# Expert gates read from DRAM in groups of eight tiles of 1 KB rows instead of groups of four of 512 B rows

## The reference, cut to what matters

```
s = einsum('thpd,hpnd->thpn', q, subkeys);  sv, si = top_k(s, 16)
comb = sv[:, :, 0, :, None] + sv[:, :, 1, None, :];  cs, ci = top_k(comb, 16)
idx = ia * 128 + ib;   g = softmax(cs)
a = einsum('td,thkd->thk', x, u_tab[idx])
out = einsum('thk,thkd->td', g * gelu(a), v_tab[idx])
```

## Time and profile before

| what | value |
|---|---|
| median of three runs | 1352.08 us (1351.38 to 1352.24) |
| profiled execution, its own time | 1351.97 us |
| its span in the trace | 1350.0 us |
| TensorE matmul busy | 1286.9 us (95%) |
| VectorE busy | 1187.2 us (88%) |
| ScalarE busy | 656.2 us (49%) |
| GpSimd busy | 612.1 us (45%) |
| DMA | 401.89 MB in 153,605 packets, mean 298 GB/s |

### The profile page before, as it was taken

The page is one execution under the profiler, slowest core; times in us unless marked ns, Lnnn a source line. Parts: engine busy times, 40 slices in busy tenths (PEclk is TensorE's granted clock), DMA queues, the critical chain, the costliest instruction groups (busy, mean ns, idle before and its releaser), DMA issues.

```text
span 1350.0 us, 22753 instructions
## 1 busy us (share of the span) xinstructions
PE 1286.9 (95%) x7713; PEld 716.5 (53%) x7713; DVE 1187.2 (88%) x2416; ACT 656.2 (49%) x927; POOL 612.1 (45%) x379
## 2 busy tenths in 40 slices
PE   6999999998865999999989999999999999999997
PEld 3554555455543667777755555555544444444444
DVE  8866398899998999999959989989999898887997
ACT  5652645465534677777634333434343333343442
POOL 4741233466741443344436656757664545222402
PEclk9999999999987999999999999999999999999999
DMA  7232422268765799999999999999999999999972
GB/s 294 95 110 68 136 79 78 94 204 280 236 229 181 264 364 389 388 394 384 407 398 351 394 393 376 400 401 382 364 384 387 375 391 381 391 385 345 386 244 105
DMA packets 153605, 401.89 MB, mean 298 GB/s; under 512 B 12352, under 2 KB 72000, under 8 KB 151360
## 3 DMA queue, kind: packets, MB, share of 16 engines
q1 hardware_dynamic: 112064, 250.06, 51.4%
q0 software_dynamic: 41472, 151.01, 28.9%
HBM read 357.51 MB, written 42.99 MB: 297 GB/s over the span
## 4 chain that ended last, share of the span: by engine, by line
PE 61%; DVE 19%; DMA 10%; issue 7%; ACT 2%; SPq 1%; DVEq 0%; ACTq 0%
PE bank L768 23%; PE bank L756 9%; PE bank L757 9%; PE bank L758 9%; DMA area<-gelu_scratch 3%; DMA raw<-tiles_dram 3%; DMA area<-gates_scratch 2%; PE bank L1033 2%; DVE cut L1442 2%; PE bank L783 2%; DVE ple_gate L1925 1%; DVE area L1686 1%; DVE area L1677 1%; DMA gates_scratch<-area 1%; DVE cut L1449 1%
## 5 line engine op out<-in xcount | busy, mean ns | idle before, releaser
L768 PE MATMUL bank<-cut,area 128*128 128x512 f16 x2208 | 485.0, 380 | 7.4 <-DVE area L1918 5.6
L756 PE MATMUL bank<-hT,cut 128*128 128x352 f16 (+1 forms) x1216 | 395.8, 326 | 34.0 <-DVE cut L1442 25.4
L757 PE MATMUL bank<-hT,cut 128*128 128x352 f16 (+1 forms) x1216 | 395.3, 325 | 0.0
L758 PE MATMUL bank<-hT,cut 128*128 128x352 f16 (+1 forms) x1216 | 395.2, 325 | 0.0
L1064 ACT ACTIVATE cut<-raw 128x1024 f16<-128x1024 f32 x246 | 257.4, 1054 | 233.5 <-DMA raw<-tiles_dram 197.2
L768 PEld LDWEIGHTS bank<-cut,area 128*128 128x128 f16 x2208 | 215.9, 98 | 265.4 <-DVE area L1918 6.2
L1442 DVE SCALAR_TENSOR_TENSOR cut<-raw,cut 128x1024 f16<-128x1024 f32 x198 | 250.2, 1265 | 44.5 <-ACT cut L1064 44.2
L756 PEld LDWEIGHTS bank<-hT,cut 128*128 128x128 f16 x1216 | 119.6, 98 | 114.7 <-DVE cut L1442 25.7
L758 PEld LDWEIGHTS bank<-hT,cut 128*128 128x128 f16 x1216 | 119.8, 98 | 76.6
L757 PEld LDWEIGHTS bank<-hT,cut 128*128 128x128 f16 x1216 | 119.7, 98 | 75.5 <-issue 0.3
L638 POOL DMA_INDIRECT ple_sb<-u_rows_dram,expert_id x64 | 103.5, 1617 | 109.3 <-DVE dots L1653 90.8
(11 more groups left out here) (223 smaller groups left out, 1648.6 us busy)
## 6 DMA issues: line engine op xcount, KB each, us to landing
raw<-tiles_dram SPq DMA_DIRECT2D x298, 512.0 KB, 6.1
gates_scratch<-area SPq DMA_DIRECT2D x12, 2048.0 KB, 11.4
area<-gates_scratch SPq DMA_DIRECT2D x32, 768.0 KB, 10.6
gelu_scratch<-gelu_out SPq DMA_DIRECT2D x80, 192.0 KB, 5.4
area<-gelu_scratch SPq DMA_DIRECT2D x20, 768.0 KB, 11.8
norm_rows<-norms_dram SPq DMA_DIRECT2D x3, 1024.0 KB, 7.7
hn<-x_dram SPq DMA_DIRECT2D x4, 512.0 KB, 4.9
out_dram<-hn SPq DMA_DIRECT2D x3, 512.0 KB, 2.6
```

Source lines behind the costliest of these rows:

```text
L756: nc.tensor.matmul(dst, w[0], hT[:, 0, k, 0:width], start=(k == 0), stop=False)
L757: nc.tensor.matmul(dst, w[0], hT[:, 1, k, 0:width], start=False, stop=False)
L758: last = nc.tensor.matmul(dst, w[1], hT[:, 0, k, 0:width], start=False, stop=(k == KD - 1))
L768: mm = nc.tensor.matmul(bank[:, 2 * tt + h, :], lhs(a)[:, tt * P:(tt + 1) * P], cut[:, t.slot, b, h * HALF:(h + 1) * HALF], start=(first a ...
```

## The change

Gates are read for eight expert tiles at a time (`GG = 8`), so that a piece is 8 x 32 x 4 B = 1 KB. Such a group is 1.5 MB and is read in two transfers of six token chunks each; a weight waits for both (32 counts of the semaphore). There are 16 groups. Group 0 is issued, both halves, where the first group of four was; the first half of group 1 where the second group of four was, its second half in the first pair. Group e + 1 is issued in round e of the pairs at indices 1 and 3; in a late round the halves of the next round's group are issued at indices 0 and 2. GELU loads keep groups of four and indices 1 and 5 of the late rounds, but their buffers move to `picks_at`, over the picks. So GELU groups 0 and 1 may be read only when the sparse weights have been made from the picks (a new semaphore, raised by a memset on VectorE), and they are issued at indices 4 and 6 of the last round of pairs. SyncE's hardware loops over the rounds become written-out code, and so do the parities that VectorE passed.

```diff
+GG = 8
-        gelu_in = part([2, VG, TD])
-        gates_in = part([2, GCH, VG, TOK])
+        gates_in = part([2, GCH, GG, TOK])
...
+        taken[0] = picks_at
+        gelu_in = part([2, VG, TD])
...
-            def load_gates(group, first, parity):
-                at_least(sp, weight_done, VG * (group - 1))
-                sp.dma_start(gates_in[:, parity],
-                             gates_dram[:, :, bass.ds(first, VG), :].rearrange("c p e t -> p c e t")
-                             ).then_inc(gates_loaded[parity], 16)
+            def load_gates(group, half):
+                first = GG * group + U_EARLY if group < EIGHTS else GG * (group - EIGHTS)
+                chunks = slice(GCH // 2 * half, GCH // 2 * (half + 1))
+                at_least(sp, weight_done, GG * (group - 1))
+                sp.dma_start(gates_in[:, group % 2, chunks],
+                             gates_dram[chunks, :, first:first + GG, :].rearrange("c p e t -> p c e t")
+                             ).then_inc(gates_loaded[group % 2], 16)
+            def load_gelu(group):
+                at_least(sp, weight_done, N_BOTH + VG * (group - 1))
+                sp.dma_start(gelu_in[:, group % 2], gelu_dram[group]).then_inc(gelu_loaded[group % 2], 16)
...
-                    load_gates(0, U_EARLY, 0)
-            load_gates(1, U_EARLY + VG, 1)
+                    load_gates(0, 0)
+                    load_gates(0, 1)
+            load_gates(1, 0)
... (in both(e), pair p)
-                    if p % 4 == 2:
-                        s = p // 4
-                        ... load_gates(2 * e + 2 + s, U_EARLY + VG * (2 * e + 2 + s), s)
+                    if e == 0 and p == 0:
+                        load_gates(1, 1)
+                    if e and p in (1, 3):
+                        load_gates(e + 1, p // 2)
+                    if e == EIGHTS - 1 and p in (4, 6):
+                        sp.wait_ge(sparse_w_done, 1)
+                        load_gelu(p // 2 - 2)
... (ahead of round EIGHTS - 2)
-            load_gelu(0, 0)
-            load_gelu(1, 1)
... (in late(e), index j)
-                        load_gates(2 * EIGHTS + 2 * e + s + 2, VG * (2 * e + s + 2), s)
-                        load_gelu(2 * e + s + 2, s)
+                    if j in (0, 2) and e + 1 < N_LATE // GG:
+                        load_gates(EIGHTS + e + 1, j // 2)
+                    if j % 4 == 1 and 2 * e + j // 4 + 2 < STORED:
+                        load_gelu(2 * e + j // 4 + 2)
... (VectorE, behind the sparse weights)
+            nc.vector.memset(word[:], 0.0).then_inc(sparse_w_done, 1)
... (VectorE, make_weight)
-                dve.wait_ge(gates_loaded[parity], 16 * (rounds + 1))
+                dve.wait_ge(gates_loaded[group % 2], 32 * (group // 2 + 1))
```

More of the change, by code:

```diff
@@ L352, in layer @@
         assert taken[0] <= 2 * P * TOK + 2 * BATCH * NKEY
+        taken[0] = picks_at
+        gelu_in = part([2, VG, TD])
+        assert taken[0] <= AREA - 2 * D
         def halves_of(t):
@@ L405, in layer @@
         gelu_loaded = [sem(f"gelu_loaded{s}") for s in range(2)]
+        sparse_w_done = sem("sparse_w_done")
         weight_done, weight_hi, weight_lo = sem("weight_done"), sem("weight_hi"), sem("weight_lo")
@@ L522, in both @@
                 for p in range(8):
-                    t = Tile(T_BOTH + 2 + 16 * e + 2 * p) if isinstance(e, int) else Tile(T_BOTH + 2 + 2 * p, 16, e)
+                    t = Tile(T_BOTH + 2 + 16 * e + 2 * p)
                     if t.c < T_LATE - 2:
@@ L526, in both @@
                         load(t.plus(1 + LOAD_AHEAD))
-                    if p % 4 == 2:
-                        s = p // 4
[L529 to L532, removed]
+                    if e == 0 and p == 0:
[5 more added lines that the diff above has]
+                        load_gelu(p // 2 - 2)
             for j in range(VG):
                 sp.wait_ge(gelu_stored[j], 16 * STORED)
-            with sp.Fori(0, EIGHTS - 2) as e:
+            for e in range(EIGHTS):
                 both(e)
-            load_gelu(0, 0)
-            load_gelu(1, 1)
-            both(EIGHTS - 2)
-            both(EIGHTS - 1)
             for n in range(T_LATE - 2, T_LATE):
@@ L545, in late @@
             def late(e):
-                fixed = isinstance(e, int)
                 for j in range(8):
-                    t = Tile(T_LATE + 8 * e + j) if fixed else Tile(T_LATE + j, 8, e)
-                    if not fixed or t.n + LOAD_AHEAD < T_ALL:
+                    t = Tile(T_LATE + 8 * e + j)
+                    if t.n + LOAD_AHEAD < T_ALL:
                         load(t.plus(LOAD_AHEAD))
-                    if j % 4 == 1 and not fixed:
-                        s = j // 4
-                        load_gates(2 * EIGHTS + 2 * e + s + 2, VG * (2 * e + s + 2), s)
-                        load_gelu(2 * e + s + 2, s)
[L555 to L559, removed]
+                    if j in (0, 2) and e + 1 < N_LATE // GG:
+                        load_gates(EIGHTS + e + 1, j // 2)
+                    if j % 4 == 1 and 2 * e + j // 4 + 2 < STORED:
+                        load_gelu(2 * e + j // 4 + 2)
+            for e in range(N_LATE // 8):
                 late(e)
-            late(N_LATE // 8 - 2)
-            late(N_LATE // 8 - 1)
             sp.wait_ge(rows_used, EXTRA + 2 * HK)
@@ L1887, in _, with make_weight @@
             dve.wait_ge(ones_done, 2)
-            def make_weight(i, slot, parity, rounds, values, ready, target):
-                dve.wait_ge(gates_loaded[parity], 16 * (rounds + 1))
+            def make_weight(i, values, ready, target):
+                group, slot = i // GG, i % RING
+                dve.wait_ge(gates_loaded[group % 2], 32 * (group // 2 + 1))
                 dve.wait_ge(ready, target)
@@ L1896, in make_weight @@
                     values.rearrange("p (c t) -> p c t", t=TOK),
-                    gates_in[:, parity, :, slot, :], ALU.mult).then_inc(weight_done, 1)
+                    gates_in[:, group % 2, :, i % GG, :], ALU.mult).then_inc(weight_done, 1)
             def make_both(e, q):
-                i = 8 * e + q
-                make_weight(i, q % RING, (q // 4) % 2, e + q // 8, gelu_out[:, q % VG, :], columns_out,
-                            N_IN + N_Q + U_EARLY + i + 1)
+                make_weight(8 * e + q, gelu_out[:, q % VG, :], columns_out, N_IN + N_Q + U_EARLY + 8 * e + q + 1)
             def make_late(e, q):
[L1907 to L1910, removed]
+                n = 8 * e + q
+                if n >= N_LATE - U_KEPT:
+                    make_weight(N_BOTH + n, gelu_kept[:, q % 8, :], columns_out, N_IN + N_Q + U_EARLY)
                     return
-                make_weight(N_BOTH + 8 * e + q, q % RING, parity, EIGHTS + rounds,
-                            gelu_in[:, parity, q % VG, :], gelu_loaded[parity], 16 * (rounds + 1))
+                make_weight(N_BOTH + n, gelu_in[:, n // VG % 2, n % VG, :], gelu_loaded[n // VG % 2],
+                            16 * (n // (2 * VG) + 1))
             def weight_low(i, slot):
```

## The result

The changed kernel takes 1376.95 us (median of four runs, 1376.31 to 1379.13) against 1351.73 for the kernel before on the same chip: a ratio of 1.0184, 95% interval 1.0166 to 1.0203. That is 25 us slower, where I had forecast no change (1352.4, range up to 1358.0).

A forecast was written before the change was run, and what follows sets the result against it. It took TensorE, with full DMA engines beside it, as the bound, with only six pauses behind 700 us to win back. Profiled 1351.97 + 1.8 - 0.5 - 1.0 + 0 gave 1352.3, 1352.4 on the median's scale; range 1349.5 to 1358.

The forecast's parts named there:

- What bounds the kernel: Whole kernel: TensorE and the DMA engines are both full; behind 700 us only six TensorE pauses can be won back.
- Price of a piece: Gate reads: a 1 KB piece costs 47.2 ns against 28.0 for 512 B, taking 13.5 us off the DMA engines.
- rival E: Whole change: 1 KB costs 56 ns, DMA work is unchanged, first pause grows 2.7 us, late pauses stay; 1354.3 us; 12%.
- Edit 1, the first group: First weight's gate load: 1,536 pieces of 1 KB in place of 512 B lengthen the first pause by 1.8 us.
- The restart of the clock: Behind the first pause: TensorE's half-speed stretch costs the same 1.3 us as before; it could vanish or double.
- Edits 2 and 3: Group 1 and pair-stage gate loads cost nothing; moving the first GELU groups removes the pause at 911.96, -0.5 us.
- Edit 4: Late rounds: one VectorE wait of 2.8 us replaces two of 1.8 in eight tiles; half of four pauses go, -1.0 us.
- queue sum: Late rounds: 3.93 MB plus 0.3 to 0.4 MB at some 254 GB/s takes 17.5 to 18 us from the first issue.
- A check of the same sum: Kernel before, late stage: the sum gives a 1.9 us wait against a mean of 1.8, so no correction was made.
- rival B: Late stage: the second gate half becomes the pacing wait; at 4.9 us it costs 5 us more, about 1358; 20%.
- My own bound for this edit: Late rounds: a 13 us landing on a 7.1 us deadline gives a wait of 5.9 us, +15 us in all.

The follow-up runs named there:

- e9_kept8: Kernel of e1_early with four of the twelve dot products beside the last eight u tiles moved into the rounds of pairs; 1344.03 us, 0.9945 of the kernel before.
- e3_512: Changed kernel, same order and halves, but each gate half read in two transfers of four expert tiles, in 512 B pieces; 1385.98 us, 1.0233 of the kernel before.
- e4_gelu_only: Kernel before with its gate loads kept; GELU buffers over the picks, GELU groups 0 and 1 in last round of pairs, loops written out; 1351.69 us, 0.9994.
- e1_early: Changed kernel, late gate halves issued at index 6 of the round before and index 0, in place of 0 and 2; 1352.74 us, 0.9992 of the kernel before.
- e2_index1: Changed kernel, second gate half of a late round issued at index 1, ahead of the GELU group, in place of 2; 1355.93 us, 1.0018 of the kernel before.
- e7_fours_later: Kernel of e4_gelu_only with late-round gate and GELU loads issued at indices 2 and 6 in place of 1 and 5; 1381.83 us, 1.0224 of the kernel before.
- e6_no_late_gathers: Changed kernel with the 84 row gathers of the late rounds left out, a probe only; 1350.81 us, 0.9988 of the kernel before.

## Why the prediction was wrong, step by step

**What bounds the kernel.** Right: TensorE is the bound, and its pauses count, with the slower clock behind the long ones; e9_kept8 shows what is left without them.

**Price of a piece.** Right: 47.2 ns forecast, 46.5 read in one stretch, and a median of 46 and a mean of 49.6 over all pieces, well under rival E's 56. The rule of 512 B for line rate (the Trainium skill, DMA: Bandwidth & Descriptors, Specifications) does not hold in these runs: 290 GB/s with pieces of 512 B, 392 GB/s with pieces mostly of 1 KB (the stretch in experiment 3).

**Edit 1, the first group.** Its mechanism was right, and the pause of 7.0 us lies at the lower edge of the 7 to 8 forecast. The load takes 20.59 us from issue to landing in place of 19.75, and it was issued at 689.17 in place of 686.96:

```profile
689.17 20.59 DMA area<-gates_scratch
```

From the first half's issue at 688.74 to the landing it is 21.0 us, so 1.3 us more where I had 1.8. The rest of the 3 us by which the landing is late is the later issue; eight runs with nothing changed ahead of it issue at 686.4 to 689.3, so it need not be the change. The restart of the clock was forecast at 1.3 us and came so, near enough: in the 3.5 us behind the pause nine products start where full speed would start 16, so 7 x 0.216 = 1.5 us.

```profile
711.50:715.00 3.50, 3.45 (x9) 1.25 (x10) 2.84 (x7) 2.33 (x4) 0.00 (x0) 0.51 0.80 284
```

**Edits 2 and 3.** Right: no pause between 711 and 1010 us, and e4_gelu_only is level.

**Edit 4 is the step that failed**, in one term: "a wait of 2.5 to 3.0 us, and I take 2.8". The wait is 7.8 us. The place at index 1 is free, as I said: there is one wait in eight tiles. VectorE's arrival (7.1 us after the issue forecast, 7.3 measured) and its work were right too. The landing was wrong: 9.9 us after the issue forecast, 14.7 to 15.8 measured in the four nine-row rounds. Two numbers of the queue sum are off. From the first half's issue to the landing, q1 moved 4.80 MB, not 4.2 to 4.3 (3.93 and a rest of 0.3 to 0.4), and in 21.7 us:

```profile
DMA packets 3341, 8.33 MB, mean 384 GB/s; under 512 B 220, under 2 KB 1756, under 8 KB 3340
...
q1 hardware_dynamic: 2377, 4.80, 58.9%
q0 software_dynamic: 963, 3.52, 42.8%
```

That is 221 GB/s for q1 where I had taken 254, or some 240 with the time of the 1 KB pieces in it. The gathers move 162 GB/s, about the 160 that I gave them; the total is 384 and not the 414 of a stretch in which all pieces are of 4 KB. The kernel before had the same rate to read: from 1040.7 us, where its gate group is issued, to VectorE's product at 1054.90 q1 moved 3.12 MB in 14.2 us, 220 GB/s.

```profile
q1 hardware_dynamic: 2120, 3.12, 62.2%
```

The larger number of bytes has its cause in the trace too. From 1039.85 to 1041.7 us no packet of q1 moves, so its queue is empty there, with one tile just issued (1040.14):

```profile
q0 software_dynamic: 103, 0.41, 76.4%
```

From there to the issue of the second half SP issues four tiles, so 512 packets of 4 KB. By the landing of that half at 1065.41, q1 has moved 716 of them. The other 204, or 0.84 MB, belong to the two tiles issued behind the half at 1053.21 and 1056.48. The rest from before, which I had put at 0.3 to 0.4 MB, is 15 packets.

A check of the same sum on the kernel before had come out right (1.9 against 1.8 us), and I let it vouch for a burst nearly twice as large (3.93 MB in place of 2.10). It was a weak check: 31.9 us over 18 groups hide that there were 15 waits, one of 3.71 us. I had also seen the slow landings of 13 us and set the limit at 3.6 us of waiting, so rival B was the right one, at 20% and with too low a price: I priced it at a wait of 4.9 us. My own bound for this edit, +15 us from a landing of 13 us, would have been 1367; the range ended at 1358, and the landing went past 13 us.

Shown by experiment: the place of the issue makes the loss (e1_early, e2_index1, e7_fours_later), sharing with the gathers makes the landing long (e6_no_late_gathers), and neither the group's size (e1_early has groups of eight and no loss, e7_fours_later groups of four and a loss) nor the size of the pieces (e3_512) makes it. Not shown: which part of the 15 us is the later tiles overtaking and which the lower total rate. At 221 GB/s the 0.84 MB are 3.8 us, an estimate and an upper bound: the trace here does not say which of the 16 engines moved them, and an engine that was done with its share of the half could serve them at no cost.

## What to carry to other kernels

Where an in-order engine waits for a transfer that is issued when it reaches an earlier step, the round is landing time plus the work from use to the next issue; compare that with the bound engine's round before moving the issue, and take the landing from the whole burst in front of it, on the engines as they are shared. Here a transfer made cheaper cost 25 us when its issue came one step nearer to its use, and nothing when it did not (e1_early). Moving other work into the freed time gave the only gain (e9_kept8, 0.55% below the kernel before), but how much of that gain the cheaper transfers carry is open.

## What the runs showed of the hardware that I had not expected

With the gathers left out, SP's 768 KB GELU loads land in 5.0 us (median), in the changed kernel in 8.9. A TensorE pause of some 4 us costs more than its own length: behind the wait of 3.81 us that ends at 1032.23 in the changed kernel the granted clock was low for a part of the stretch,

```profile
1028.00:1036.00 8.00, 4.19 (x12) 1.43 (x11) 5.99 (x8) 3.06 (x4) 1.01 (x1) 0.79 0.69 256
```

while behind the pause of 2.49 us that ends at 1067.66 it stayed at 1.00 (1064 to 1073). The 144 products of a round show the price, 32.94 us behind the longer pause and 31.41 behind the shorter:

```profile
1032.23 32.94 PE L766 MATMUL bank<-cut,area 128*128 128x512 f16 x144 [3.81 <-DVE cut L1440]
1067.66 31.41 PE L766 MATMUL bank<-cut,area 128*128 128x512 f16 x144 [2.49 <-DVE cut L1440]
```

The six waits of 18.9 us therefore account for less than the 24 us of products that were not started.
